# The feature sums of squares of three RMS norms, summed on TensorE as two single-pass products of a split operand

## The reference: what is computed

```python
def rms_norm(x, g):
    xf = x.astype(jnp.float32)
    y = xf * lax.rsqrt(jnp.mean(xf * xf, axis=-1, keepdims=True) + RMS_EPS)
    return (y * g.astype(jnp.float32)).astype(x.dtype)
...
    for i in range(DEPTH):
        j = i // 2
        if i % 2 == 0:
            h = h + mla_mixer(rms_norm(h, mla_norm[j]), positions, mla_w_in[j],
                              mla_g_cq[j], mla_g_ckv[j], mla_w_uq[j], mla_w_ukv[j], mla_w_o[j])
        else:
            h = h + short_conv_mixer(rms_norm(h, conv_norm[j]), conv_w_in[j],
                                     conv_w[j], conv_w_out[j])
        h = h + swiglu(rms_norm(h, ffn_norm[i]), ffn_w_gate[i], ffn_w_up[i], ffn_w_down[i])
    return rms_norm(h, final_norm)
```

## Time and profile before

| | |
|---|---|
| median of 3 runs | 1063.45 us (1062.01 to 1063.56) |
| the profiled execution, its own time | 1061.74 us |
| its span, first to last instruction | 1060.0 us |
| PE busy | 1051.7 us, 99% |
| PEld, DVE, ACT, POOL busy | 954.8 us, 846.2 us, 529.2 us, 41.8 us |
| granted TensorE clock | full in every slice |
| HBM traffic | 100 GB/s over the span |

### The profile page before, as it was taken

How to read it: one execution, slowest core, us unless ns; L and a number is a source line. 1 busy time by engine, 2 the same in 40 slices (tenths; PEclk the granted TensorE clock), 3 DMA queues, 4 the chain that set the end, 5 groups by cost and what they waited for, 6 DMA issues and landing times.

```text
span 1060.0 us, 17801 instructions
## 1 busy us (share of the span) xinstructions
PE 1051.7 (99%) x6766; PEld 954.8 (90%) x6766; DVE 846.2 (80%) x1195; ACT 529.2 (50%) x755; POOL 41.8 (4%) x24
## 2 busy tenths in 40 slices
PE   9999999999999999999999999999999999999998
PEld 8888888899999999888888888888999999988997
DVE  6777775999999998634678677689999999898675
ACT  6688873745554555421443323365445545563332
POOL 0232230000000000000000000000000000000000
PEclk9999999999999999999999999999999999999999
DMA  8121112233223323223223232222332233232212
GB/s 338 51 70 50 67 53 80 80 120 119 85 113 119 102 96 109 92 97 109 107 82 116 83 117 83 86 114 80 119 119 91 107 119 109 79 110 101 92 67 80
DMA packets 16967, 106.21 MB, mean 100 GB/s; under 512 B 1888, under 2 KB 2272, under 8 KB 6432
## 3 DMA queue, kind: packets, MB, share of 16 engines
q1 hardware_dynamic: 16560, 104.86, 27.5%
q10 hardware_dynamic: 288, 0.56, 0.2%
q0 software_dynamic: 80, 0.26, 0.1%
HBM read 103.59 MB, written 2.10 MB: 100 GB/s over the span
## 4 chain that ended last, share of the span: by engine, by line
PE 95%; DVE 2%; ACT 1%; issue 1%; DMA 0%; DVEq 0%
PE bank L502 31%; PE bank L503 31%; PE bank L504 31%; PE bank L669 1%; ACT split L1228 1%; DMA first_raw<-weights_in 0%; PE bank L657 0%; PE bank L655 0%; DVE s_lo L1826 0%; PE bank L541 0%; PE bank L576 0%; DVE mid_lo L1510 0%; PE bank L911 0%; PE bank L923 0%; PE bank L555 0%
## 5 line engine op out<-in xcount | busy, mean ns | idle before, releaser
L502 PE MATMUL bank<-x_hi,split 128*128 128x256 f32 (+1 forms) x704 | 204.1, 290 | 0.0
L503 PE MATMUL bank<-x_lo,split 128*128 128x256 f32 (+1 forms) x704 | 203.4, 289 | 0.0
L504 PE MATMUL bank<-x_hi,split 128*128 128x256 f32 (+1 forms) x704 | 203.4, 289 | 0.0
L957 ACT ACTIVATE split<-raw 128x2048 fp32r<-128x2048 f32 (+2 forms) x51 | 90.1, 1766 | 136.2 <-PE bank L504 136.1
L1467 DVE TENSOR_TENSOR split<-raw,split 128x2048 fp32r<-128x2048 f32 (+2 forms) x43 | 92.5, 2152 | 59.2 <-ACT split L957 59.1
L502 PEld LDWEIGHTS bank<-x_hi,split 128*128 128x128 f32 x704 | 132.3, 188 | 3.0 <-issue 0.5
L503 PEld LDWEIGHTS bank<-x_lo,split 128*128 128x128 f32 x704 | 132.3, 188 | 3.0 <-issue 0.5
L502 PE MATMUL bank<-x_hi,s_hi 128*128 128x256 f32 x480 | 134.3, 280 | 0.6 <-ACT work L1238 0.6
L504 PEld LDWEIGHTS bank<-x_hi,split 128*128 128x128 f32 x704 | 132.3, 188 | 2.5
L503 PE MATMUL bank<-x_lo,s_hi 128*128 128x256 f32 x480 | 133.8, 279 | 0.0
L504 PE MATMUL bank<-x_hi,s_lo 128*128 128x256 f32 x480 | 133.8, 279 | 0.0
(11 more groups left out here) (280 smaller groups left out, 2209.4 us busy)
## 6 DMA issues: line engine op xcount, KB each, us to landing
raw<-weights_in SPq DMA_DIRECT2D x82, 1024.0 KB, 4.8
raw<-weights_in SPq DMA_DIRECT2D x12, 768.0 KB, 4.2
work<-x SPq DMA_DIRECT2D x4, 512.0 KB, 12.6
raw<-weights_in SPq DMA_DIRECT2D x4, 512.0 KB, 3.7
out<-head SPq DMA_DIRECT2D x3, 512.0 KB, 2.7
head<-head_in SPq DMA_DIRECT2D x1, 768.0 KB, 9.0
first_raw<-weights_in SPq DMA_DIRECT2D x3, 192.0 KB, 5.1
first_raw<-weights_in SPq DMA_DIRECT2D x1, 576.0 KB, 7.7
```

Of the source, the lines that this page charges most:

```text
L502: pe.matmul(o, lhs[0], rhs[0], start=start, stop=False, skip_group_check=True)
L503: pe.matmul(o, lhs[0], rhs[1], start=False, stop=False, skip_group_check=True)
L504: return pe.matmul(o, lhs[1], rhs[0], start=False, stop=stop, skip_group_check=True)
L957: act.activation(w_hi[s][:, 0:n], raw[s][:, 0:n], ACT.Copy).then_inc(hi_split[s], 1)
```

## The change

`stat` no longer multiplies `ones` by the float32 tile `acc` in one float32 matmul. `acc` is split first: ACT copies it to a float32r tile `acc_hi` (`acc_high_part`), DVE writes `acc - acc_hi` to a float32r tile `acc_lo` (`acc_rest`), and PE multiplies a float32r `ones` by each, adding both in the bank. PE waits for the semaphore `acc_split` of DVE's subtraction where it waited for the last addition. In the gate and up stages DVE's subtraction stands between `split` and `x_rest_of(c, 1)`; in the convolution stage it stands behind `forms(0)`. On ACT the copy stands ahead of `idle_sqrt` in all three.

```diff
-        ident, ones = sb("ident", P), sb("ones", P)
+        ident, ones_r = sb("ident", P), sb("ones", P, F32R)
+        ones = ones_r[:, :].bitcast(F32)
+        acc_hi, acc_lo = (placed(n, SUMS_AT[1] + (4 + i) * TILE_BYTES, SEQ) for i, n in enumerate(("acc_hi", "acc_lo")))
...
+        acc_high, acc_split = sem("acc_high"), sem("acc_split")
...
             def stat(b, tiles):
 
-                if tiles:
-                    pe.wait_ge(squares_added, T.add("added", tiles))
+                T.add("added", tiles)
+                pe.wait_ge(acc_split, T.add("acc"))
                 open_bank(b)
-                pe.matmul(bank[b][:, :], ones[:, :], acc[:, :], start=True, stop=True).then_inc(stat_summed, 1)
+                pe.matmul(bank[b][:, :], ones_r[:, :], acc_hi[:, :], start=True, stop=False, skip_group_check=True)
+                pe.matmul(bank[b][:, :], ones_r[:, :], acc_lo[:, :], start=False, stop=True, skip_group_check=True).then_inc(stat_summed, 1)
...
+            def acc_high_part():
+
+                act.wait_ge(squares_added, T.now("added"))
+                act.activation(acc_hi[:, :], acc[:, :], ACT.Copy).then_inc(acc_high, 1)
...
             def ffn(layer):
+                acc_high_part()
                 idle_sqrt()
                 rms(4, D)
...
             ffn(0)
+            acc_high_part()
             idle_sqrt()
             T.add("x", K_PAIRS)
             act.wait_ge(stat_summed, T.add("stat"))
...
+            def acc_rest():
+
+                v.wait_ge(acc_high, T.add("acc"))
+                v.tensor_tensor(acc_lo[:, :], acc[:, :], acc_hi[:, :], ALU.subtract).then_inc(acc_split, 1)
...
                     if c == K_PAIRS - 1:
                         split(c % 2)
+                        acc_rest()
                     x_rest_of(c, 1)
...
             forms(0)
+            acc_rest()
             conv_tail_rest(3)
             done(0)
             forms_split(0)
```

## The result

The changed kernel takes 1065.28 us (median of 7 runs, 1064.95 to 1066.98) against 1061.79 us (1061.59 to 1063.56) for the kernel before in the same comparison: a ratio of 1.0033, 95% interval 1.0023 to 1.0043. It is slower by about 3.5 us. The profiled executions say 1065.04 and 1061.74 us, with spans of 1063.2 and 1060.0 us: 3.2 us.

The account below looks back on a forecast made before the run. The prediction took PE's stream of matmuls, busy 99% of the span, as the bound. It summed +2.5 - 0.2 - 0.4 = +1.9 us, giving 1063.6 to 1065.4 us by baseline, and took 1065.0, range 1063.0 to 1068.0.

Parts of the forecast that it names:

- the sum: Whole kernel: +2.5 in the convolution, -0.2 and -0.4 in the gate and up stages, together +1.9 us.
- What PE saves: At each of three stats, two 0.226 us matmuls replace one 0.87 us product: 0.42 us saved, 1.25 in all.
- The rule read for a whole product: Skill's halved TensorE rate for FP32_LOW_HIGH, applied to the whole stat: 0.45 us for it, saving zero.
- The convolution's stat: PE waits 2.79 us for DVE's subtraction, which stands behind the four operations of forms(0).
- The net of +2.5 us: Convolution: wait +2.79, slower first matmul +0.11, cheaper products -0.42 us.
- nothing would be given back later: Behind the convolution's stat no PE wait is there to shrink, so the 2.5 us stay.
- The gate and up stages: No wait, or a tenth, before either stat; DVE's queue 0.61 us later; 0.2 us saved in the first, 0.4 in the second.
- the pricing of the clock: Rival, chance 0.11: clock falls to 1.2 GHz behind the convolution's wait, adding 2.8 us, +4.7 in all, 1068.1 us.
- a slow stretch of twice the wait: Clock rival's chosen size: 5.6 us at half pace behind the convolution's wait, adding 2.8 us.
- a stretch as long as the wait: Clock rival's other size: half pace for as long as the convolution's wait, adding 1.4 us.
- The rival that gives back nothing in the gate stages: DVE's later queue eats PE's gain there: +2.5 to +2.9, 1065.6 to 1066.2 us; chance 0.22 with products that save nothing.
- The rival without a wait: Convolution's subtraction done by 552.24, only PE's saving counts: -1.2 or -1.0, 1062.4 us; chance 0.09.

Follow-up runs that it names:

- early order: Changed kernel with the convolution's ACT copy ahead of conv_tail_hi(3) and DVE subtraction ahead of conv_tail_rest(2) and conv_forms(3): 1060.84 us, ratio 0.9977 to the kernel before.
- order ahead of `forms(0)`: Changed kernel with the convolution's DVE subtraction ahead of forms(0), ACT's copy left behind conv_tail_hi(3): 1064.36 us, ratio 1.0017.
- added DVE operation: Early order plus one unused 128x512 DVE operation behind the subtraction in both gate and up stages: 1062.24 us, ratio 1.000.
- first profile: First profiled execution of the changed kernel itself, nothing altered: 1065.04 us, span 1063.2 us.
- filler: Changed kernel with eleven thrown-away 512-column matmuls ahead of the convolution's stat: median 1064.70 us, ratio 1.0013; profiled twice, spans 1063.6 and 1062.0 us.
- part alone: Changed kernel with split sums in the two gate and up stages only, old float32 stat in the convolution: 1061.70 us, ratio 0.9988.

## Why the prediction was right or wrong

The predicted range, 1063.0 to 1068.0, holds 1065.28, and the predicted time, 1065.0, is near it. But that nearness is partly luck: the sum was +1.9 us on a level of 1063.1, and the comparison gave +3.5 on 1061.8. The direction was left to same and slower at about even odds; it is slower, by a third of a percent.

**What PE saves.** Worked out as 0.42 us each. From the last matmul ahead of the stat to the third behind it there are 1.55 us before (212.81 to 214.36) and 1.16 after (212.94 to 214.10): 0.39. Right. The rule read for a whole product, by which there was nothing to save, is refuted by the same numbers.

**The convolution's stat.** A wait of 2.79 us was predicted and 2.79 measured, for the named reason: order on DVE. (As the profile counts it, 2.63, it lies just under the 2.7 to 2.9 that the prediction named for the profile.) The early order and the order ahead of `forms(0)` each moved it as worked out, to nothing and to 1.86. The net of +2.5 us is 2.46 in the execution whose clock stayed up. That nothing would be given back later held as well, though ACT's high halves moved by 1.9 us (554.81 to 556.70) and not by 1.5.

**The gate and up stages.** No wait ahead of either stat: right, with 0.01 us of room by the sum and 0.07 in the trace (the subtraction ends at 212.84, PE loads at 212.95, less the 0.04 of the release). Of the saving, 0.27 and 0.43 us came through where 0.2 and 0.4 were forecast, and the wait at 239 us grew from 0.28 to 0.45. In the changed kernel `forms(1)` ends at 227.93 and ACT's high blocks start at 227.97, where 227.86 and about 227.9 were worked out. The added DVE operation shows that it is DVE's queue, through `forms(1)` and ACT's high blocks, that takes the rest.

**Where it was wrong.** The step that failed is the pricing of the clock, treated as a rival with a chance of 0.11 and +2.8 us. It belongs into the sum: it came in 9 of 14 executions, and in the first profile it costs 1.36 us, half of what was set for it. The prediction had set a slow stretch of twice the wait; its other figure, a stretch as long as the wait, gives the right 1.4. With 1.36 in the sum, +1.9 becomes +3.3, which is the measured 3.2 of span. A fall of the clock was also on the prediction's own list of what would show it wrong. The prediction had no row on a wait of this length and let the rival stand at the chance of something unlikely. The Trainium skill (TensorE: Matmul & The Clock Gate, Why this matters for your kernels) warns of idle gaps between bursts of matmuls, and that was the better guide than the silence of the trace. The runs agree with the page that a gap can bring half rate, and the filler shows that it is the gap; that a gap of 2.8 us brings it in some executions and not in others, the runs alone show.

The rival that gives back nothing in the gate stages is refuted by the part alone (-0.8 us). The rival without a wait did not occur in the change, but it is what the early order made: -1.0 us was its price, and 1.0 was measured.

## What to carry to other kernels

When a product is made cheaper by preparing its operand on other engines, the preparation's place in their queues is the price, not its duration: ask at what time the last queue ahead of it is through, and compare with the moment at which TensorE arrives. Here 0.7 us of DVE work cost 2.8 us in one place, up to 0.2 in another, and nothing once it stood where its inputs were ready. Put the clock's share into the sum as soon as an edit makes a busy TensorE stand still for some microseconds, with both outcomes; and where a stand cannot be removed, matmuls whose result is thrown away can be cheaper than the stand.

## What the runs showed of the hardware

- Read from the mean granted clock of each execution, TensorE's clock fell to 1.2 GHz at a stand of 2.8 us in 9 of 14 executions of one kernel and 6 of 10 of another, at one 1.1 us longer in 4 of 4, at one 0.9 us shorter in 0 of 10, and in 0 of 11 where matmuls filled the 2.8 us. In one kernel and at one place, so, the same wait may or may not cost the 1.36 us.
- A 128x512 subtraction on POOL took 2.61 us beside DVE's 2.28 us operation, and made DVE's next one 1.09 us longer.
- Executions of the same kernel lie 1.7 us apart in levels. In the two profiles on a slower level the excess grows evenly over the block rounds of one feed-forward stage and is nowhere else: from 239 to 423 us in the filler's first (set against its second), from 750 to 934 us in the one with the added DVE operation (set against the early order), both at full granted clock. Why was not found.
